# Down-projection end, softmax units and output projection reordered in a gated FFN plus two attention layers on one core

## The chip, the core and the metric

The kernel runs on one NeuronCore of a Trainium2 chip. The metric is the time of one execution on the device, in microseconds (us). Five engines work side by side and wait for each other through semaphores: TensorE (PE) does matmuls, VectorE (DVE) and ScalarE (ACT) elementwise work and reductions, GpSimd (POOL) a few set-ups, SyncE (SP) issues the loads. PE writes to PSUM (8 banks of 128 x 512 float32); DVE and ACT read it.

## What is computed

512 tokens of width 1024 go through a first block (a recurrent token mixer, then a gated FFN with a causal convolution) and then through two layers of three attention branches:

```python
# first block, FFN part
f = causal_dwconv(hn @ w_up) + b;  gate, up = split(f)
ffn = (gelu(gate) * up) @ w_down                  # 2816 -> 1024
h = h + rms_norm(ffn, post_ffn_g)
# each of two layers
h = rms(x, norm_g);  proj = h @ w_in
log_a = log_sigmoid(a_lr @ wa2 + ba) / 16         # 16 -> 256, decay of the linear attention
y_a = linear attention * silu(gz)
y_b = sparse attention (top keys by an indexer) * silu(bz)
y_c = (softmax(Q1 K1) - lambda softmax(Q2 K2)) V, normed, * silu(cz)
merged = sum of sigmoid(gate_b) * (y_b @ w_br[b]) over the three branches
x = x + merged @ w_out
```

## The kernel before

Every large matmul is done in float32r as three products: each operand is split into a high part and a low part (the rest), and high x high, low x high and high x low are summed in PSUM. So each weight panel (up to 128 x 2048 elements) goes through three steps: SP loads it to `w_raw`; ACT copies it to `w_hi` (`split_hi`, L347); DVE subtracts and writes `w_lo` (`split_lo`, L365). All three tiles have two slots, used in turn by the panel's number. `w_hi` of a panel can be written only after PE is done with the panel two before it, PE takes a panel only when its `w_lo` is there, and SP loads into a slot once the low part of its former panel is made.

The order of work on each engine is written out by hand, one function per engine and stage; an engine takes its list strictly in order. The helpers `high(p)` and `low(p)` put the two splits of panel p into ACT's and DVE's lists. The stages that matter here:

**FFN end** (`ffn`). The down projection has 11 panels. ACT, for each: `split_hi` of the panel, then the high part of the hidden values (`g hi`, L1776). DVE: `g lo` (L1820), then `split_lo`. The last two panels are worked by PE token tile by token tile (L1719), and a seam follows that norms the result and starts layer 0.

**Decay bias** (`layer`). The low-rank values stand in `lowrank_iw`, 24 rows: 16 of the decay, 8 index weights. For each of four token tiles PE multiplies the 16 rows by `gla_wa2` (L2236) and adds the bias by a matmul with one row of ones (L2237).

**Softmax loops** (`layer`). Two per layer, 16 units each (a head and a query tile of 128, with 4, 3, 2, 1 key tiles visible), first for the difference attention ("d"), then for the sparse one ("s"). PE, at unit u: transposes the probabilities of u, makes the logits of u + 2, computes one tile of a merge panel as filling, multiplies u's probabilities with the values. DVE: maximum of u + 1 (`softmax_max`), in the first loop one step of a top-k search, normalisation of u + 1 (`softmax_norm`), gating of a branch tile, and after odd units the low part of the panel two ahead. ACT: copy of the transposed probabilities (L2461), high parts at odd units, exponentials (L2447), head output (L2468). ACT keeps its functions in tables that have to be loaded on a change (ACT_TABLE_LOAD).

**Output projection** (`first_out`). `outs[0]` is the first of four panels of `w_out`; PE goes through it by rows of the merged values as their low parts (`merged lo`, L3021) come. ACT makes eight `merged hi` copies (L2659); the last two depend on the gating of the last merge panel by DVE (L2801, L2807).

```python
for i in range(2):
    gated(mergeB + 7, i)
    merged_lo(KT - 2 + i)
low(outs[1])
```

Of the kernel before, what the change touches and what calls it, by code (L numbers as in the profile page):

```python
# [72 lines left out]
SHARED = ("seam", "w raw", "w hi", "w lo", "w used")  # L73
# [267 lines left out]
def split_hi(act, m, g, n):  # L341

    act.wait_ge(*act.point(("w raw", g)))
    act.wait_ge(act.done, act.so_far())
    if g >= 2:
        act.wait_ge(act.sems["pe"], act.at(("w used", g - 2)))
    act.eng.activation(m.wh[:, g % 2, 0:n], m.raw[:, g % 2, 0:n], ACT.Copy).then_inc(act.done, 1)  # L347
    act.counted(("w hi", g))

# [1277 lines left out]
def ffn(m, A, done, sems, seam, after, base):  # L1627
# [120 lines left out]
    def scalar(E):  # L1748
        act = E.eng
        post_sum(E, m, seam, 0)  # L1750
        pre_sum(E, m, seam, 0)
        post_sum(E, m, seam, 1)
        split_hi(E, m, base, PANEL)
        pre_sum(E, m, seam, 1)
        seam_hi(E, m, seam, 0)
        post_sum(E, m, seam, 2)
        seam_hi(E, m, seam, 1)
        post_sum(E, m, seam, 3)
        split_hi(E, m, base + 1, PANEL)
        pre_sum(E, m, seam, 2)  # L1760
        pre_sum(E, m, seam, 3)
        seam_hi(E, m, seam, 2)
        seam_hi(E, m, seam, 3)
        for p in range(FT):
            E.wait_ge(act_done, E.so_far())
            if p >= 2:
                E.wait_ge(dve_done, E.at(("G", p - 2)))
            E.wait_ge(dve_done, E.at(("conv", p, 0)))
            act.activation(m.gel[:, p % 2, :], m.cgu[:, p % 2, 0, :], ACT.Gelu_apprx_tanh).then_inc(act_done, 1)
            E.counted(("gelu", p))  # L1770
            split_hi(E, m, base + p + 2, PANEL)
        for kk in range(2, DN):
            split_hi(E, m, down_base + kk, PANEL)
            E.wait_ge(act_done, E.so_far())
            E.wait_ge(dve_done, E.at(("G", 2 * kk + 1)))
            act.activation(m.gH[:, kk % 2, :, :], m.G[:, 2 * kk:2 * kk + 2, :], ACT.Copy).then_inc(act_done, 1)  # L1776
            E.counted(("g hi", kk))
        seam_table(E, m, after)

    def vector(E):  # L1780
# [36 lines left out]
        for kk in range(2, DN):  # L1817
            E.wait_ge(dve_done, E.so_far())
            E.wait_ge(act_done, E.at(("g hi", kk)))
            dve.tensor_tensor(m.gL[:, kk % 2, :, :], m.G[:, 2 * kk:2 * kk + 2, :], m.gH[:, kk % 2, :, :].bitcast(F32),  # L1820
                              ALU.subtract).then_inc(dve_done, 1)
            E.counted(("g lo", kk))
            split_lo(E, m, down_base + kk, PANEL)
# [12 lines left out]
RANK = 16  # L1836
TAU = 16.0
# [5 lines left out]
def lay_out_layers(nc, m):  # L1843
# [35 lines left out]
    m.lw = take("lowrank_iw", [RANK + IH, T], over=q + 24 * KB)  # L1879
# [10 lines left out]
    m.wa2 = take("gla_wa2", [RANK, 256], over=pt)  # L1890
    m.ba = take("gla_ba", [1, 256], over=pt + KB)
# [3 lines left out]
    m.sc = take("index_scores", [P, P * sum(range(2, TT + 1))])  # L1895
    m.later = m.bd
# [12 lines left out]
def layer(m, A, out, done, sems, l, base, seam, after):  # L1909
# [102 lines left out]
    def sync(E):  # L2012
        sp = E.eng

        def rows_in():
# [12 lines left out]
            sp.dma_start(m.wa2[:, :], A["gla_wa2_2"][l, :, :]).then_inc(small_loaded, 16)  # L2028
            sp.dma_start(m.ba[:, :], A["gla_ba_2"][l:l + 1, :]).then_inc(small_loaded, 16)
# [32 lines left out]
    def gpsimd(E):  # L2062
# [7 lines left out]
        if l == 0:  # L2070
            E.wait_ge(pe_done, E.before(None, ("y mean", JT - 1)))
            E.wait_ge(dve_done, E.before(None, ("conv", FT - 1, 1)))
            step(pool.affine_select(out=m.later[:, :], in_=m.later[:, :], compare_op=ALU.is_gt, fill=0.0, base=0,
                                    pattern=[[-1, P]], channel_multiplier=1), "later 3")
            for i in range(2):
                step(pool.memset(m.lamc[:, i, 0:1], LAMBDA[i]), ("lambda 0", i))
                step(pool.memset(m.lamc[:, i, 1:2], 1.0 - LAMBDA[i]), ("lambda 1", i))

    def tensor(E, banks):
# [148 lines left out]
        turn(E, m, banks, "turn iw", 6, "iw", [m.lw[:, P * t:P * t + P] for t in range(TT)],  # L2228
             rows=RANK + IH)
        E.wait_ge(*E.point("small"))  # L2230
        for g in range(2):
            o = start(("z", g), 4 + g, ("la", g))
            for q in range(2):
                t = 2 * g + q
                oo = o[:, 256 * q:256 * q + 256]
                pe.matmul(oo, m.lw[0:RANK, P * t:P * t + P], m.wa2[:, :], start=True, stop=False)  # L2236
                last = pe.matmul(oo, m.onesP[0:1, :], m.ba[:, :], start=False, stop=True)  # L2237
# [140 lines left out]
    def scalar(E):  # L2378
# [6 lines left out]
        def evac(p, i):  # L2385
# [5 lines left out]
            if p == lows:  # L2391
# [4 lines left out]
                ins = act.activation(m.lw[:, :], PS[64:64 + RANK + IH, b, :], ACT.Copy)  # L2396
# [202 lines left out]

        exps(0, "d", (0, 1), 64 ** -0.5)  # L2600
# [50 lines left out]
        for p in range(mergeB, mergeB + 7):  # L2651
# [4 lines left out]
        for j in range(KT):  # L2656
# [3 lines left out]
            E.counted(("merged hi", j))  # L2660
        high(outs[1])
        high(outs[2])
# [4 lines left out]
    def vector(E):  # L2667
# [280 lines left out]
        step(cz[1])  # L2948
        softmax_max(0, "d")
        softmax_norm(0, "d")  # L2950
        softmax_max(1, "d")
        softmax_norm(1, "d")
        for u in range(1, NU):
            p, i = mergeA + u // 2, u % 2
            if u + 1 < NU:
                softmax_max(u + 1, "d")
            top(18 + u, 19 + u)
# [4 lines left out]
            if i:  # L2962
                low(p + 2)
# [38 lines left out]
        for u in range(1, NU):  # L3002
            p, i = mergeC + u // 2, u % 2
            if u + 1 < NU:
                softmax_max(u + 1, "s")
                softmax_norm(u + 1, "s")
            if panels[p].name == "br":
                gated(p, i)
            if i:
                low(p + 2)  # L3010
# [19 lines left out]
        low(outs[0])  # L3030
        for j in range(KT - 2):
            merged_lo(j)
        for i in range(2):
            gated(mergeB + 7, i)
            merged_lo(KT - 2 + i)
# [103 lines left out]
```

## Time and profile before

| what | value |
|---|---|
| median of three timed runs | 2007.99 us (2002.96 to 2009.97) |
| profiled execution, its own time | 1997.83 us |
| its span | 1996.1 us |
| PE busy | 1918.2 us, 96% |
| weight loads on PE | 1543.2 us, 77% |
| DVE busy | 1144.9 us, 57% |
| ACT busy | 744.9 us, 37% |
| POOL busy | 54.2 us, 3% |
| 16 DMA engines, queue of the weights | 25.8% of their span, 159.00 MB |
| granted TensorE clock, mean | 0.989 of full |

The profile is one execution as the hardware recorded it; busy times are per engine and overlap. A line such as "745.72 0.47 PE L1719 ... [1.49 <-DVE w_lo L365]" gives the start, the length, the engine, the code line, the operation with what it writes and reads, and in brackets how long the engine was idle before it and which event ended that.

### The profile page before, as it was taken

What the parts mean: (1) busy time and instruction counts of PE and PEld (TensorE: products, weight loads), DVE (VectorE), ACT (ScalarE), POOL (GpSimd) and SP (SyncE); (2) the same over time, 40 slices, a digit from 0 to 9 for tenths busy, and PEclk for the clock granted to TensorE, in tenths of its full rate; (3) what the DMA queues carried; (4) which work ended last, traced back from release to release, by engine and by line L of the source; (5) the groups of instructions that cost most, each with busy time, mean ns of one, the idle gap of its engine ahead of it and who ended that gap; (6) DMA issues with size and microseconds to landing.
All of it is one profiled execution on the core that took longest, in us unless ns stands there. A gap on an engine that the chain in (4) does not pass through costs nothing.

```text
span 1996.1 us, 30217 instructions
## 1 busy us (share of the span) xinstructions
PE 1918.2 (96%) x12657; PEld 1543.2 (77%) x12657; DVE 1144.9 (57%) x1684; ACT 744.9 (37%) x1063; POOL 54.2 (3%) x75
## 2 busy tenths in 40 slices
PE   6989998899999999999999999999999999999998
PEld 4767775888888878787777778878778777778887
DVE  3674345476766236446687855454446678775533
ACT  5532422432222226433444334333543344334431
POOL 3000000310000000000000000000000000000000
PEclk9999998999999999999999999999999999999999
DMA  4221003233333232222222212233222312232232
GB/s 145 77 64 45 25 24 112 65 84 106 85 106 98 93 112 86 67 85 85 64 64 85 90 59 84 74 100 101 85 78 70 95 57 82 73 96 64 64 106 84
DMA packets 166034, 161.63 MB, mean 81 GB/s; under 512 B 13892, under 2 KB 150378, under 8 KB 165898
## 3 DMA queue, kind: packets, MB, share of 16 engines
q1 hardware_dynamic: 165200, 159.00, 25.8%
q8 instruction: 99, 1.62, 0.3%
q10 hardware_dynamic: 698, 0.71, 0.1%
q14 instruction: 37, 0.30, 0.0%
HBM read 157.59 MB, written 2.10 MB: 80 GB/s over the span
## 4 chain that ended last, share of the span: by engine, by line
PE 69%; DVE 6%; ACT 3%; issue 1%; ACTq 0%; DVEq 0%
PE psum L557 57%; PE psum L1719 5%; DVE w_lo L365 2%; PE psum L2203 1%; ACT w_hi L347 1%; PE psum L547 1%; PE psum L2160 1%; PE psum L2188 1%; DVE softmax_stats L2758 1%; ACT probs L2447 1%; PE psum L2180 1%; PE psum L495 1%; DVE h_lo L3021 0%; PE psum L504 0%; DVE probs L2789 0%
## 5 line engine op out<-in xcount | busy, mean ns | idle before, releaser
L557 PE MATMUL psum<-h_hi,w_hi 128*128 128x512 f32 (+2 forms) x1592 | 624.6, 392 | 15.9 <-DVE h_lo L429 7.4
L557 PE MATMUL psum<-h_lo,w_hi 128*128 128x512 f32 (+2 forms) x1592 | 607.8, 382 | 0.0
L557 PE MATMUL psum<-h_hi,w_lo 128*128 128x512 f32 (+2 forms) x1592 | 607.8, 382 | 0.0
L365 DVE TENSOR_TENSOR w_lo<-w_raw,w_hi 128x2048 fp32r<-128x2048 f32 (+2 forms) x147 | 306.7, 2086 | 367.4 <-ACT w_hi L347 365.0
L347 ACT ACTIVATE w_hi<-w_raw 128x2048 fp32r<-128x2048 f32 (+2 forms) x157 | 276.5, 1761 | 397.9 <-PE psum L557 318.9
L557 PEld LDWEIGHTS psum<-h_hi,w_hi 128*128 128x128 f32 (+1 forms) x1592 | 300.7, 189 | 96.0 <-issue 13.6
L557 PEld LDWEIGHTS psum<-h_hi,w_lo 128*128 128x128 f32 (+1 forms) x1592 | 300.7, 189 | 58.3
L557 PEld LDWEIGHTS psum<-h_lo,w_hi 128*128 128x128 f32 (+1 forms) x1592 | 301.3, 189 | 53.9
L557 PE MATMUL psum<-w_hi,h_hi 128*128 128x512 f32 (+1 forms) x512 | 183.3, 358 | 7.5 <-DVE w_lo L365 4.0
L557 PE MATMUL psum<-w_lo,h_hi 128*128 128x512 f32 (+1 forms) x512 | 179.9, 351 | 0.0
L557 PE MATMUL psum<-w_hi,h_lo 128*128 128x512 f32 (+1 forms) x512 | 179.8, 351 | 0.0
L557 PEld LDWEIGHTS psum<-w_hi,h_hi 128*128 128x128 f32 x512 | 97.8, 191 | 36.0 <-issue 11.4
L557 PEld LDWEIGHTS psum<-w_hi,h_lo 128*128 128x128 f32 x512 | 97.8, 191 | 12.8
L557 PEld LDWEIGHTS psum<-w_lo,h_hi 128*128 128x128 f32 x512 | 97.9, 191 | 11.7
L557 PE MATMUL psum<-y_hi,w_hi 128*128 128x512 f32 x192 | 80.2, 418 | 0.0
L2447 ACT ACTIVATE probs<-psum,softmax_stats 128x128 f32<-128x128 f32 (+3 forms) x72 | 36.1, 506 | 113.8 <-DVE softmax_stats L2773 113.8
L557 PE MATMUL psum<-y_hi,w_lo 128*128 128x512 f32 x192 | 75.2, 392 | 0.0
L557 PE MATMUL psum<-y_lo,w_hi 128*128 128x512 f32 x192 | 75.2, 391 | 0.0
L1804 DVE TENSOR_SCALAR ffn_conv<-psum,ffn_cols 128x512 f32<-128x512 f32 x44 | 35.6, 810 | 63.3 <-PE psum L557 62.2
L1719 PE MATMUL psum<-w_hi,ffn_hi 128*128 128x512 f32 x176 | 68.8, 391 | 2.0 <-DVE w_lo L365 1.5
L1719 PE MATMUL psum<-w_lo,ffn_hi 128*128 128x512 f32 x176 | 68.5, 389 | 0.0
L1719 PE MATMUL psum<-w_hi,ffn_lo 128*128 128x512 f32 x176 | 68.5, 389 | 0.0
(339 smaller groups left out, 2128.5 us busy)
## 6 DMA issues: line engine op xcount, KB each, us to landing
w_raw<-in_w_in_dram SPq DMA_DIRECT2D x170, 512.0 KB, 4.5
w_raw<-in_w_up_dram SPq DMA_DIRECT2D x44, 512.0 KB, 4.7
w_raw<-in_w_out_dram SPq DMA_DIRECT2D x24, 512.0 KB, 4.5
w_raw<-in_w_br_dram SPq DMA_DIRECT2D x48, 256.0 KB, 2.9
w_raw<-in_w_down_dram SPq DMA_DIRECT2D x22, 512.0 KB, 4.3
x_first<-in_x_dram SPq DMA_DIRECT2D x4, 512.0 KB, 5.2
x_tokens<-in_x_dram SPq DMA_DIRECT2D x4, 512.0 KB, 6.6
out_dram<-x_tokens SPq DMA_DIRECT2D x4, 512.0 KB, 2.6
```

Of the source, the lines that this page charges most:

```text
L347: act.eng.activation(m.wh[:, g % 2, 0:n], m.raw[:, g % 2, 0:n], ACT.Copy).then_inc(act.done, 1)
L365: eng.eng.tensor_tensor(m.wl[:, g % 2, 0:n], m.raw[:, g % 2, 0:n], m.wh[:, g % 2, 0:n].bitcast(F32), ALU.subtract).then_inc(eng.done, 1)
L495: last = pe.eng.matmul(out[q, :], m.ind[:, kind, q], x[:, j, :], start=begin, stop=end, skip_group_check=True)
L547: last = pe.eng.transpose(m.PS[0:n, bank, rows * i:rows * i + rows], b, m.ident[at:at + rows, at:at + rows])
L557: last = pe.eng.matmul(out, a(k), b(k), start=(opens and k == 0 and i == 0), stop=(k == kt - 1 and i == 2), skip_group_check=ks is not None)
L1719: last = pe.matmul(PS[:, 2 * t + n, :], g[:, kk % 2, k, tt], w[:, k, cc], start=(kk == 0 and k == 0 and i == 0), stop=(kk == DN - 1 and k ...
L1804: dve.tensor_scalar(c, z, tap[2], bias, ALU.mult, ALU.add).then_inc(dve_done, 1)
L2160: pe.matmul(o[:, 0:vis], m.Q[r, h // 2, P * i:P * i + P], m.ikf[r, 0:vis], start=True, stop=True).then_inc(pe_done, 1)
L2180: last = pe.matmul(o[:, 0:vis], m.Q[r, h, P * i:P * i + P], m.K[r, h, 0:vis], start=True, stop=True)
L2188: pe.matmul(o[:, 0:vis], m.Q[:, h, P * i:P * i + P], m.K[:, h, 0:vis], start=True, stop=True).then_inc(pe_done, 1)
L2203: last = pe.matmul(o[:, 0:P], m.V[:, k, P * h:P * h + P], m.PT[:, u % 2, P * k:P * k + P], start=(k == 0), stop=(k == i))
L2447: ins = act.activation(dst, src, ACT.Exp, bias=m.st[:, u % 2, 2 + c:3 + c], scale=scale, accum_out=m.st[:, u % 2, 4 + c:5 + c])
```

## The change

- FFN: the weights of the last down panel are split in two halves on ACT and on DVE (`split_hi_halves`, `split_lo_halves`), and on ACT the high part of the hidden values goes ahead of them; it gets a wait of its own for the down panel two before it.
- Layers, decay bias: `lowrank_iw` and `gla_wa2` get 32 rows and places of their own. Rows 24 to 31 of the first are ones; of the second, row 24 is the bias and the others beyond 16 are zero. One matmul in place of two. POOL clears both once, in layer 0, and SP waits for that.
- First softmax loop: an exponential of two columns is put right behind the last evacuation, so that the table is loaded there; DVE waits for it. The low part of panel `mergeA + 1` moves behind the first maximum.
- Both loops: low parts move from after odd units into the following even unit, between maximum and normalisation.
- Output projection: first panel in halves; the high part of the second panel moves ahead of the last two merged copies, and DVE makes both last gatings before the last two low parts.

```diff
+def split_hi_halves(act, m, g, n):
+    act.wait_ge(*act.point(("w raw", g)))
+    if g >= 2:
+        act.wait_ge(act.sems["pe"], act.at(("w used", g - 2)))
+    for half in range(2):
+        c = slice(n // 2 * half, n // 2 * (half + 1))
+        act.wait_ge(act.done, act.so_far())
+        act.eng.activation(m.wh[:, g % 2, c], m.raw[:, g % 2, c], ACT.Copy).then_inc(act.done, 1)
+        act.counted(("w hi", g) if half else ("w hi half", g))
+def split_lo_halves(dve, m, g, n):
+    for half in range(2):
+        c = slice(n // 2 * half, n // 2 * (half + 1))
+        dve.wait_ge(dve.done, dve.so_far())
+        dve.wait_ge(dve.sems["act"], dve.at(("w hi", g) if half else ("w hi half", g)))
+        dve.eng.tensor_tensor(m.wl[:, g % 2, c], m.raw[:, g % 2, c], m.wh[:, g % 2, c].bitcast(F32),
+                              ALU.subtract).then_inc(dve.done, 1)
+        dve.counted(("w lo", g) if half else ("w lo half", g))
...
         for kk in range(2, DN):
-            split_hi(E, m, down_base + kk, PANEL)
+            if kk < DN - 1:
+                split_hi(E, m, down_base + kk, PANEL)
             E.wait_ge(act_done, E.so_far())
             E.wait_ge(dve_done, E.at(("G", 2 * kk + 1)))
+            E.wait_ge(pe_done, E.at(("dn mm", kk - 2)))
             act.activation(m.gH[:, kk % 2, :, :], m.G[:, 2 * kk:2 * kk + 2, :], ACT.Copy).then_inc(act_done, 1)
             E.counted(("g hi", kk))
+        split_hi_halves(E, m, down_base + DN - 1, PANEL)
...
-            split_lo(E, m, down_base + kk, PANEL)
+            if kk < DN - 1:
+                split_lo(E, m, down_base + kk, PANEL)
+        split_lo_halves(E, m, down_base + DN - 1, PANEL)
...
-            sp.dma_start(m.wa2[:, :], A["gla_wa2_2"][l, :, :]).then_inc(small_loaded, 16)
-            sp.dma_start(m.ba[:, :], A["gla_ba_2"][l:l + 1, :]).then_inc(small_loaded, 16)
+            if l == 0:
+                E.wait_ge(pool_done, E.at("low ones"))
+            sp.dma_start(m.wa2[0:RANK, :], A["gla_wa2_2"][l, :, :]).then_inc(small_loaded, 16)
+            sp.dma_start(m.wa2[LOWS:LOWS + 1, :], A["gla_ba_2"][l:l + 1, :]).then_inc(small_loaded, 16)
...
+            step(pool.memset(m.wa2[:, :], 0.0), "low zeros")
+            step(pool.memset(m.lw[:, :], 1.0), "low ones")
...
-                pe.matmul(oo, m.lw[0:RANK, P * t:P * t + P], m.wa2[:, :], start=True, stop=False)
-                last = pe.matmul(oo, m.onesP[0:1, :], m.ba[:, :], start=False, stop=True)
+                last = pe.matmul(oo, m.lw[:, P * t:P * t + P], m.wa2[:, :], start=True, stop=True)
...
+        E.wait_ge(act_done, E.so_far())
+        act.activation(m.st[:, 0, 2:4], m.eps[:, :], ACT.Exp).then_inc(act_done, 1)
+        E.counted("exp table")
         exps(0, "d", (0, 1), 64 ** -0.5)
...
-        for p in range(mergeB, mergeB + 7):
+        for p in range(mergeB, mergeB + 6):
...
-        for j in range(KT):
+        gate(mergeB + 6, 0)
+        gate(mergeB + 6, 1)
+        split_hi_halves(E, m, base + outs[0], size(outs[0]))
+        for j in range(KT - 2):
+            merged_hi(j)
         high(outs[1])
+        merged_hi(KT - 2)
+        merged_hi(KT - 1)
...
-        step(cz[1])
+        E.wait_ge(act_done, E.at("exp table"))
         softmax_max(0, "d")
+        low(mergeA + 1)
         softmax_norm(0, "d")
...
             if u + 1 < NU:
                 softmax_max(u + 1, "d")
+            if i == 0:
+                low(p + 1)
             top(18 + u, 19 + u)
             if u + 1 < NU:
                 softmax_norm(u + 1, "d")
             if panels[p].name == "br":
                 gated(p, i)
-            if i:
-                low(p + 2)
+        low(bq[1])
...
-        low(outs[0])
+        split_lo_halves(E, m, base + outs[0], size(outs[0]))
         for j in range(KT - 2):
             merged_lo(j)
         for i in range(2):
             gated(mergeB + 7, i)
-            merged_lo(KT - 2 + i)
+        merged_lo(KT - 2)
+        merged_lo(KT - 1)
```

## Rows read from the trace of the kernel before

**Rows 1.** The page, busy us of each engine with its share of the span.
```profile
PE 1918.2 (96%) x12657; PEld 1543.2 (77%) x12657; DVE 1144.9 (57%) x1684; ACT 744.9 (37%) x1063; POOL 54.2 (3%) x75
```
**Rows 2.** Timeline of PE, FFN end: start, length, what, idle before.
```profile
743.84 0.39 PE L1719 MATMUL psum<-w_lo,ffn_hi 128*128 128x512 f32 x1
745.72 0.47 PE L1719 MATMUL psum<-w_hi,ffn_hi 128*128 128x512 f32 x1 [1.49 <-DVE w_lo L365]
```
**Rows 3.** Timeline of ACT, FFN end.
```profile
738.91 1.92 ACT L347 ACTIVATE w_hi<-w_raw 128x2048 fp32r<-128x2048 f32 x1 [7.87 <-PE psum L1719]
740.86 1.06 ACT L1776 ACTIVATE ffn_hi<-ffn_hidden 128x1024 fp32r<-128x1024 f32 x1
...
743.23 0.20 ACT L400 ACTIVATE row_stats<-eps 128x1 f32<-128x1 f32 x1
```
**Rows 4.** Groups by shape, 984:1084, DVE low part of 128x1024: busy, mean ns.
```profile
L365 DVE TENSOR_TENSOR w_lo<-w_raw,w_hi 128x1024 fp32r<-128x1024 f32 x4 | 4.9, 1226 | 7.0 <-ACT w_hi L347 6.9
```
**Rows 5.** Timeline of PE, decay matmuls of layer 0 and the panel behind.
```profile
790.16 0.59 PE L2236 MATMUL psum<-gla_wa,lowrank_iw 16*128 16x256 f32 x2
790.59 0.59 PE L2237 MATMUL psum<-gla_ba,ones 1*128 1x256 f32 x2
791.69 0.79 PE L557 MATMUL psum<-h_hi,w_hi 128*128 128x512 f32 x1 [0.51 <-DVE w_lo L365]
```
**Rows 6.** Timelines of DVE, ACT and PE, start of the first softmax loop.
```profile
986.81 0.17 DVE L2750 MEMSET psum<- 64x128 f32 x1
...
988.51 1.28 ACT L2447 ACT_TABLE_LOAD   x1 [2.50 <-DVE softmax_stats L2773]
...
992.95 0.66 PE L547 MATMUL psum<-ident,probs 128*128 128x128 f32 x4 [1.37 <-DVE probs L2789]
```
**Rows 7.** Timelines of DVE and PE, unit 2 of that loop.
```profile
1003.83 2.29 DVE L365 TENSOR_TENSOR w_lo<-w_raw,w_hi 128x2048 fp32r<-128x2048 f32 x1 [3.12 <-ACT w_hi L347]
...
1008.92 0.35 DVE L2789 SCALAR_TENSOR_TENSOR probs<-probs,softmax_stats 128x128 f32<-128x128 f32 x1
...
1009.77 0.27 PE L547 MATMUL psum<-ident,probs 128*128 128x128 f32 x1
```
**Rows 8.** Timelines of DVE and PE, end of that loop.
```profile
1076.15 2.29 DVE L365 TENSOR_TENSOR w_lo<-w_raw,w_hi 128x2048 fp32r<-128x2048 f32 x1 [2.27 <-ACT w_hi L347]
...
1079.40 0.69 DVE L2712 MAX8 top<-index_scores 128x8 f32<-128x512 f32 x1
...
1081.04 0.71 PE L2203 MATMUL psum<-probs_t,v_toks 128*128 128x128 f32 x4 [1.56 <-ACT probs_t L2461]
1081.90 0.33 PE L547 MATMUL psum<-ident,probs 128*128 128x128 f32 x1
```
**Rows 9.** Timeline of PE, end of the second loop.
```profile
1263.91 0.71 PE L2203 MATMUL psum<-probs_t,v_toks 128*128 128x128 f32 x4 [0.43 <-ACT probs_t L2461]
```
**Rows 10.** Timelines of ACT, DVE and PE, output projection of layer 0.
```profile
1326.51 1.92 ACT L347 ACTIVATE w_hi<-w_raw 128x2048 fp32r<-128x2048 f32 x1
...
1330.86 4.32 DVE L3021 TENSOR_TENSOR h_lo<-merged,h_hi 128x512 fp32r<-128x512 f32 x6
...
1331.69 0.47 PE L557 MATMUL psum<-w_hi,h_hi 128*128 128x512 f32 x1 [0.52 <-DVE h_lo L3021]
...
1336.72 0.63 ACT L2659 ACTIVATE h_hi<-merged 128x512 fp32r<-128x512 f32 x1 [4.31 <-DVE merged L2807]
...
1344.86 0.47 PE L557 MATMUL psum<-w_hi,h_hi 128*128 128x512 f32 x1 [2.00 <-DVE w_lo L365]
```
**Rows 11.** Windows of PE: stretch, its us, PE busy, granted clock, DMA share, GB/s.
```profile
788.00:791.40 3.40, 3.18 (x15) 1.00 0.00 0
791.40:794.80 3.40, 3.11 (x7) 0.50 0.59 175
...
1402.40:1409.20 6.80, 6.80 (x17) 0.50 0.68 229
...
1695.90:1699.30 3.40, 3.40 (x11) 0.50 0.00 1
```

More of the change, by code:

```diff
@@ L70, in __init__ @@
         self.w = sum(c[2] for c in pieces)
-SHARED = ("seam", "w raw", "w hi", "w lo", "w used")
+SHARED = ("seam", "w raw", "w hi half", "w hi", "w lo half", "w lo", "w used")
 class Steps:
@@ L1836 @@
 RANK = 16
+LOWS = RANK + IH
 TAU = 16.0
@@ L1878, in lay_out_layers @@
     m.ikf = take("ik_feats", [P, T], over=q + 8 * KB)
-    m.lw = take("lowrank_iw", [RANK + IH, T], over=q + 24 * KB)
     o = at[0]
@@ L1889, in lay_out_layers @@
     m.rn3 = take("norm_rows3", [P, T], over=pt)
-    m.wa2 = take("gla_wa2", [RANK, 256], over=pt)
-    m.ba = take("gla_ba", [1, 256], over=pt + KB)
     m.lam_in = take("lambda_in", [P, 4, 64], over=pt + 2 * KB)
@@ L1895, in lay_out_layers @@
     m.sc = take("index_scores", [P, P * sum(range(2, TT + 1))])
+    m.lw = take("lowrank_iw", [LOWS + LOWS // 3, T])
+    m.wa2 = take("gla_wa2", [LOWS + LOWS // 3, 256])
     m.later = m.bd
@@ L2227, in tensor @@
         E.wait_ge(act_done, E.at(("Levac", lows, 0)))
-        turn(E, m, banks, "turn iw", 6, "iw", [m.lw[:, P * t:P * t + P] for t in range(TT)],
+        turn(E, m, banks, "turn iw", 6, "iw", [m.lw[0:LOWS, P * t:P * t + P] for t in range(TT)],
              rows=RANK + IH)
@@ L2395, in evac @@
                 E.counted("ik high")
-                ins = act.activation(m.lw[:, :], PS[64:64 + RANK + IH, b, :], ACT.Copy)
+                if l == 0:
+                    E.wait_ge(pool_done, E.at("low ones"))
+                ins = act.activation(m.lw[0:LOWS, :], PS[64:64 + LOWS, b, :], ACT.Copy)
             elif panels[p].tokens:
@@ L2655, in scalar, with merged_hi @@
             high(p + 2)
-        for j in range(KT):
+        def merged_hi(j):
             E.wait_ge(act_done, E.so_far())
@@ L3005, in vector @@
                 softmax_max(u + 1, "s")
+            if i == 0:
+                low(p + 1)
+            if u + 1 < NU:
                 softmax_norm(u + 1, "s")
@@ L3008, in vector @@
                 gated(p, i)
-            if i:
-                low(p + 2)
+        low(mergeB + 1)
         for h in range(NH):
```

## The prediction

> **What bounds the kernel now.** I read the page's busy times first: TensorE (PE) is busy for 1918.2 of a 1996.1 us span [rows 1]. So only two things can shorten the run: fewer PE instructions on its path, or shorter pauses between them. I then went through PE's timeline for pauses in the three stages that the change touches, and at each one looked at ACT and DVE in the same microseconds for the step that ended it. The pauses sit at handovers: end of the down projection, start and end of each softmax loop, and the output projection. Each gap, as shown, is 0.16 us short of what it costs: a matmul is drawn 0.39 us long, but in the steady stream the next one starts after 0.23 us [rows 2]. I count gap + 0.16.
>
> **End of the FFN.** The last down panel (10) needs two things from ACT: the high part of its weights (1.92 us), then that of the hidden values (1.06). DVE follows with two low parts, the second a 128x2048 of 2.29 us (as in [rows 7]). PE starts at 745.72 after 1.49 idle, so 1.65 lost [rows 2, 3]. After the change ACT starts at the same 738.91 (the new wait, on down panel 8, is the event that released ACT before): hidden high part to 739.97, weight halves to 741.06 and 742.14, each costed as the 128x1024 copy of 1.06 [rows 3]. DVE: hidden low part 740.07 to 741.30, first half 741.33 to 742.56, second half, which must wait for ACT's second half, 742.60 to 743.83, at 1.23 us each [rows 4]. PE could start at 743.97. Its stream before ends with a start at 743.84, so the natural next start is 744.07 [rows 2]: the pause goes, with 0.1 us to spare. Gain 1.65 (bounds 0 and 1.65; I take all of it, since every duration has a row of its own shape). Halving costs 0.20 us on ACT and 0.17 on DVE, already in these times. The seam behind it hangs on this panel's result, so it moves along. ACT's root table load is next and has over 3 us until its first use.
>
> **Decay bias as a row.** Per layer, four matmuls with K=1 go; each of the eight took 0.43 us from start to start, so 1.7 us of PE work per layer. But PE then waits 0.51 us anyway for the low part of the next panel, whose high part could only begin when the panel before was used [rows 5]. PE would merely arrive 1.7 us earlier and wait 2.2. In layer 1 the last of the eight ends just as that low part is ready, so again nothing is freed. Value 0; bounds 0 and 3.5 us for both layers, and nearer 0 because the waiting step has no link to the bias. The two memsets on POOL, and SP's wait for them in layer 0, lie behind the up panels and ahead of the seam, in time when POOL has nothing else; the rows and weights queued behind SP's wait are asked for later. The zero rows cost nothing in streaming: PE's time here is by columns. I have no row for K=32; bounds are the K=1 and K=16 times, both 0.43.
>
> **Exponential table early (start of the first softmax loop, in both layers).** Now: ACT evacuates until 986.01, idles 2.50, loads the table only after DVE's maximum (1.28), then exponentials; PE waits 1.37 [rows 6]. After: load 986.03 to 987.31, dummy exponential 0.20 (as the one-column operation of [rows 3]), 987.53. DVE's maximum writes the same statistics tile and so now waits for this: it starts at about 987.60 instead of 986.81 [rows 6], 0.79 later, and the 1.30 behind it goes. Net 0.51, twice 1.0. Queued behind DVE's new wait: maximum, a weight low part (1.23), the normalisation. That low part moves between maximum and normalisation and runs 989.25 to 990.47, while ACT's exponentials run to about 990.7, so it is covered; were it not, it would cost its 1.23. Bounds -1.2 and 1.53 per layer.
>
> **Low parts inside a unit (both softmax loops).** Order on DVE was low part, next maximum, normalisation; it becomes maximum, low part, normalisation. The low part waits for ACT anyway (3.12 us idle before it [rows 7]), and the maximum, 0.8 us, fits in that idle. Inside the loop PE has no pause to win. At the end of the first loop it has: DVE does the low part (begun at 1076.15, right behind ACT's high part) until 1078.44, then the maximum and its small steps until 1079.40; ACT's exponentials wait for that, the transposed probabilities come late, and PE pauses 1.56 before the values of unit 14; unit 15's transpose at 1081.90 then follows DVE's normalisation [rows 8]. After: the maximum is done before the low part, ACT is free from 1076.05, unit 14's values start without pause, and unit 15's normalisation ends 0.96 earlier, which is what remains as PE's limit. Unit 15's own path behind it is unchanged. I take 0.92 per layer, 1.8 in all (bounds 0 and 1.72 per layer). In the second loop the same pause is 0.43, cost 0.59 [rows 9], and goes whole: there the normalisation is ready when the values end. 1.2 for both layers.
>
> **Output projection.** PE pauses 0.52 before its first panel and 2.00 before its second [rows 10], that is 0.68 and 2.16. First: ACT's high part in halves from 1326.51 ends at 1328.66 instead of 1328.43, but DVE starts on the first half at 1327.67, ends both at 1330.14 and the first merged low part (0.72) at 1330.86; PE can go at 1331.0, its natural start being 1331.03. Gain 0.66. Second: the panel's high part stood behind all eight merged copies on ACT, though ACT idled 4.31 us before the seventh [rows 10]. Now it goes into this idle, 1332.65 to 1334.57 (its buffer is free when panel 7 of the merge ends at about 1331.2). DVE: five more merged low parts to 1334.5, four gating steps of 0.72 to 1337.4, low parts 7 and 8 to 1338.9, weight low part to 1341.3. PE ends the first panel at 1342.1. Gain 2.16, with 0.8 us to spare (bounds 0 and 2.16). Both layers: 5.6.
>
> **Sum.** 1.65 + 2 x (0 + 0.51 + 0.92 + 0.59 + 0.66 + 2.16) = 11.3 us. The profiled execution took 1997.83 (span 1996.1 and 1.7 around it), so 1986.5 in its terms. The three timed runs lie higher, 2002.96 to 2009.97 with median 2007.99, 10.2 above it; I carry the difference over: 1996.7.
>
> **The clock.** TensorE's granted clock was 1.00 in 788.0:791.4 and 0.50 in the 3.4 us behind it [rows 11]: the lower of its two levels, 1.2 for 2.4 GHz, and 1.7 us lost. Before this fall PE ran small matmuls almost without a gap (3.18 of 3.40 us busy).
> The Trainium skill (TensorE: Matmul & The Clock Gate, "What's actually happening") says that the engine is throttled by default and only activity lifts this, with idleness bringing it back. By that, the 2.2 us idle that the bias edit leaves speaks against the change; the trace agrees only in part, since the engine here was busy, if with few rows.
>
> **Rivals.**
> A. The falls get fewer, since pauses at loop ends shrink. The clock stood at the lower level after the decay matmuls of both layers (3.4 and 6.8 us) and after the first softmax loop of layer 1 (3.4) [rows 11]: half of 13.6 is 6.8. Then -18.1, 1990. For it: one of the three follows exactly a pause that shrinks. Against: two follow the decay matmuls, whose stretch keeps its length.
> B. The falls get more or longer: PE idle instead of working ahead of the panel, in both layers, for one or two such stretches each, 1.7 us a time: 3.4 to 6.8 back, so -4.5 to -7.9, 2000 to 2003.5. For it: idle comes in. Against: the low-activity stretch (787.1 to 791.7) is as long as before.
> C. The handovers without margin don't pay (FFN end, table, first output panel: 0.1, 0.5 and 0.03 us are small against a late semaphore): then only 2 x (0.92 + 0.59 + 2.16) = 7.3 stays, 2000.7. For it: two margins of 0.1 or less. Against: a missed margin costs only what it misses.
> D. Slower: the low part now stands in front of the normalisation, and PE's transpose waits for that. In unit 2, normalisation ended at 1009.27 and the transpose came at 1009.77: 0.5 us slack [rows 7]. If the 2.29 us low part began that much later than now, four such panels a loop and four loops would cost 16 x 1.8 = 29 us, net +17, 2025. It decides from 1.2 us of delay per unit (0.5 slack + 11.3/16). Against: the low part begins when ACT's high part is ready, in both orders; only if the maximum's logits were late would it be delayed, and they are issued two units ahead.
>
> **Numbers.** Forecast 0.60 (its own range 1992 to 2001), A 0.12, B 0.12, C 0.11, D 0.05. What a measurement of this kernel can tell from no change is about 0.3%, 6 us. Faster by more: forecast, A, most of C and half of B, less a little for the 7 us between equal runs: 0.81. Within: 0.14. Slower: 0.05. Range 1989 to 2003.5: A below, B and C above, D left out.
>
> **What would show it.** PE's gap of 1.49 before the last down panel and those of 0.52 and 2.00 before the output panels gone; 1.37 down to about 0.85 at the first loop's start; 1.56 at its end replaced by about 1.0 before unit 15's transpose; the gap behind the decay matmuls up from 0.51 to 2.2 with the next panel no earlier. Wrong, if DVE's normalisations end later inside the loops, or if the first output panel starts on time and the second still waits, or if the granted clock falls in more places than three behind the FFN.

## The result and the profile after

| | before | this change |
|---|---|---|
| median of 4 runs, us | 2006.88 (2002.96 to 2009.97) | 1984.8 (1983.99 to 1985.71) |
| profiled execution: time, span | 1997.83, 1996.1 | 1984.06, 1982.0 |
| mean granted clock, profiled | 0.989 | 0.989 |

The ratio is 0.99, interval 0.9879 to 0.992. The forecast of 1996.7 us was 11.9 too high, and the time lies below its range (1989). The two profiled executions differ by 14.1 us of span where the sum said 11.3.

The page after, for [rows 1]: busy us of each engine, and the chain that ended last by engine.

```profile
PE 1911.6 (96%) x12641; PEld 1540.9 (78%) x12641; DVE 1145.3 (58%) x1687; ACT 746.2 (38%) x1068; POOL 56.5 (3%) x77
...
PE 75%; DVE 2%; ACT 1%; issue 0%; ACTq 0%; DVEq 0%
```

On the page of before that last line reads PE 69%, DVE 6%, ACT 3%. So DVE and ACT held 9 per cent of the chain, and 3 are left. That is where the chain runs, not what was gained: 6 per cent of the span would be 120 us.

PE's timeline after (start, length, what, idle before), in the order of [rows 2, 5, 6, 8, 9, 10]:

```profile
743.89 0.39 PE L1742 MATMUL psum<-w_lo,ffn_hi 128*128 128x512 f32 x1
744.12 0.39 PE L1742 MATMUL psum<-w_hi,ffn_hi 128*128 128x512 f32 x1
...
787.99 1.97 PE L2268 MATMUL psum<-gla_wa,lowrank_iw 32*128 32x256 f32 x8
...
792.20 0.80 PE L580 MATMUL psum<-h_hi,w_hi 128*128 128x512 f32 x1 [2.25 <-DVE w_lo L388]
...
993.11 0.33 PE L570 MATMUL psum<-ident,probs 128*128 128x128 f32 x1 [0.90 <-DVE probs L2834]
...
1078.91 0.61 PE L2235 MATMUL psum<-probs_t,v_toks 128*128 128x128 f32 x4
1079.54 0.33 PE L570 MATMUL psum<-ident,probs 128*128 128x128 f32 x1
1080.29 0.49 PE L2235 MATMUL psum<-probs_t,v_toks 128*128 128x128 f32 x2 [0.43 <-ACT probs_t L2494]
...
1260.95 0.61 PE L2235 MATMUL psum<-probs_t,v_toks 128*128 128x128 f32 x4
...
1327.99 0.47 PE L580 MATMUL psum<-w_hi,h_hi 128*128 128x512 f32 x1
...
1338.96 0.39 PE L580 MATMUL psum<-w_hi,h_hi 128*128 128x512 f32 x1
```

This view leaves out the brackets where the idle time is under 0.15 us. The pauses of 1.49, 1.56, 0.43, 0.52 and 2.00 us are gone (the 0.43 shown at 1080.29, before the values of unit 15, is another one, and before has it too), 1.37 is 0.90, and 0.51 behind the decay matmuls is 2.25. Unit 15's transpose (1079.54) follows unit 14's values at once: the rest of 1.0 us that the prediction left there isn't there. The end of the FFN and the output projection, from ACT's side and then from DVE's, for [rows 3, 10]:

```profile
739.64 1.06 ACT L1801 ACTIVATE ffn_hi<-ffn_hidden 128x1024 fp32r<-128x1024 f32 x1 [7.87 <-PE psum L1742]
740.79 2.16 ACT L359 ACTIVATE w_hi<-w_raw 128x1024 fp32r<-128x1024 f32 x2
...
1323.47 2.16 ACT L359 ACTIVATE w_hi<-w_raw 128x1024 fp32r<-128x1024 f32 x2
1325.66 3.96 ACT L2696 ACTIVATE h_hi<-merged 128x512 fp32r<-128x512 f32 x6
1329.70 1.92 ACT L347 ACTIVATE w_hi<-w_raw 128x2048 fp32r<-128x2048 f32 x1
1333.02 0.63 ACT L2696 ACTIVATE h_hi<-merged 128x512 fp32r<-128x512 f32 x1 [1.40 <-DVE merged L2852]
```

```profile
740.80 1.23 DVE L1846 TENSOR_TENSOR ffn_lo<-ffn_hidden,ffn_hi 128x1024 fp32r<-128x1024 f32 x1 [5.38 <-ACT ffn_hi L1801]
742.06 2.48 DVE L369 TENSOR_TENSOR w_lo<-w_raw,w_hi 128x1024 fp32r<-128x1024 f32 x2
...
1324.63 2.48 DVE L369 TENSOR_TENSOR w_lo<-w_raw,w_hi 128x1024 fp32r<-128x1024 f32 x2 [9.04 <-ACT w_hi L359]
1327.15 4.33 DVE L3070 TENSOR_TENSOR h_lo<-merged,h_hi 128x512 fp32r<-128x512 f32 x6
```

The hidden values come first, the weights in two copies behind them, and DVE starts on the first half while ACT makes the second. The second output panel's high part now fills ACT's idle time.

**Where the 14.1 us are.** I cut PE's timeline at the same named instructions in every profiled execution. In brackets: us of the stretch at the lower granted clock, where there are any.

| stretch, us | before | after | gain |
|---|---|---|---|
| start to first down matmul | 639.9 (30.7) | 640.6 (30.7) | -0.7 |
| down projection | 123.31 | 121.60 | 1.71 |
| seam, to decay of layer 0 | 24.26 | 25.76 (3.4) | -1.50 |
| decay to first softmax loop, both layers | 394.52 (10.2) | 394.59 (10.2) | -0.07 |
| first softmax loop, both layers | 197.26 | 191.48 | 5.78 |
| first to second loop, both layers | 188.70 (3.4) | 187.08 | 1.62 |
| second softmax loop, both layers | 178.28 | 176.90 | 1.38 |
| second loop to next layer or end | 249.86 | 243.95 | 5.91 |

What is left of the difference of the spans, once the clock's falls (-1.50, +1.62), the untouched first stretch and the 0.07 of the fourth are set aside, is 15.0: 1.71 + 2 x 2.99 + 1.38 + 5.91, with the first loop of layer 1 counted as that of layer 0.

### The profile page after: what moved, and what is told of

Read it like the earlier page. It is cut to its first block, busy times and chain, and to the rows that moved or that the text cites. A ratio compares the mean times of both kernels' runs of the same rounds, so it can differ in the third digit from the quotient of the medians.

```text
span 1982.0 us, 30195 instructions
## 1 busy us (share of the span) xinstructions
PE 1911.6 (96%) x12641; PEld 1540.9 (78%) x12641; DVE 1145.3 (58%) x1687; ACT 746.2 (38%) x1068; POOL 56.5 (3%) x77
## 3 DMA queue, kind: packets, MB, share of 16 engines
q8 instruction: 99, 1.62, 0.3%
## 4 chain that ended last, share of the span: by engine, by line
PE 75%; DVE 2%; ACT 1%; issue 0%; ACTq 0%; DVEq 0%
PE psum L580 62%; PE psum L1742 5%; PE psum L2235 2%; PE psum L570 1%; PE psum L2212 1%; PE psum L2192 1%; PE psum L2220 1%; DVE w_lo L388 1%; PE psum L518 1%; ACT w_hi L347 1%; PE psum L527 0%; PE psum L2316 0%; DVE h_lo L452 0%; DVE ffn_normed L465 0%; PE psum L2301 0%; DVE x_tokens L469 0%
## 5 line engine op out<-in xcount | busy, mean ns | idle before, releaser
L388 DVE TENSOR_TENSOR w_lo<-w_raw,w_hi 128x2048 fp32r<-128x2048 f32 (+2 forms) x144 | 299.8, 2082 | 285.6 <-ACT w_hi L347 282.9
L347 ACT ACTIVATE w_hi<-w_raw 128x2048 fp32r<-128x2048 f32 (+2 forms) x154 | 270.7, 1758 | 390.9 <-PE psum L580 320.0
L2512 ACT ACTIVATE squares<-psum 128x512 f32<-128x512 f32 x48 | 28.7, 598 | 109.2 <-PE psum L580 108.8
```

The lines of the kernel that those rows point to most:

```text
L388: eng.eng.tensor_tensor(m.wl[:, g % 2, 0:n], m.raw[:, g % 2, 0:n], m.wh[:, g % 2, 0:n].bitcast(F32), ALU.subtract).then_inc(eng.done, 1)
L2512: act.activation(m.sq3[:, 2 * (r % 2) + i, :], PS[:, bank(p, i), :], ACT.Tanh, scale=0.5).then_inc(act_done, 1)
```

## The experiments

Every kernel below was timed against the kernel before on the same chip. Since the run time follows the mean granted clock of its run, I also give each kernel's distance to before at equal clock: one straight line of time against mean clock through all timed runs, with a level of its own for each kernel (slope 17.8 us per 0.01 of clock, residual 1.57 us). There were 73 runs of before beside these kernels and 12 of its repetition, 1998.0 to 2014.9 us; all 85 count as one kernel. Two limits of this measure: before's own level differs by up to 0.9 us between the three series (lowest in the one with the table, the FFN end, the third run of the change and the change without the bias row), and a fall of the clock that a kernel itself avoids is taken out with the rest.

**Before and after once more.** No edit; the change as it stands in the second and, on another occasion, a third series.

> The kernel before, unchanged, timed and profiled again. Open is why its timed runs lay 5 to 12 us above its profiled execution, while those of the changed kernel lie within 2 us of theirs. Theory 1 (the excess is a state of those runs or of that chip, not of the program): here its times come out near 1998, equal to its profile within 2 us, and the changed kernel is 12 to 15 us below it. Theory 2 (the program itself loses more clock in most executions than in the one profiled): timed runs at 2003 to 2010 again, and in single runs more time at the lower of the two clock levels.

> The whole change, timed beside the kernel before on one chip. Theory 1: 12 to 15 us faster (the spans of the two traces differ by 14.1). Theory 2: about 20 to 22 us faster, 1984 to 1986 in all runs.

> The whole change a third time, to see what a handful of runs can be worth. Theory 1 (the program gains 15.0 us at an equal granted clock, and the rest of the first result, 7 us, was the draw of the clock in four runs against four): the runs spread over 1984 to 1998 with their mean clock between 0.982 and 0.989, and fitted against the clock they lie 15 us below the kernel before. Theory 2 (the change itself makes falls of the clock rarer, and so gains 20 or more on the whole): all runs at 1984 to 1987, mean clock 0.988, while the kernel before keeps its 0.985.

Before against itself: ratio 1.0006 (0.9987 to 1.0025), its median 2006.77 (1999.0 to 2014.7), which speaks for theory 2; for the change theory 1 held both times. The change: 1990.1 us (1983.8 to 1997.3) against 2003.59, ratio 0.9927 (0.9902 to 0.9952); the third time 1988.74 against 2003.03, ratio 0.9918 (0.99 to 0.9937). At equal clock it is 14.6 and 14.9 us faster (±1.3 each), and 14.9 in the four runs of the result. So the change is worth 15 us, 0.75%. By this line the rest of the 22 us between the medians of the result is which executions were caught. This windows view shows PE busy, matmul count, granted clock, DMA share and GB/s over the first 640 us, which the change doesn't touch: before, after, then these two kernels.

```profile
0.00:640.00 640.00, 586.64 (x6064) 0.98 0.27 80
```

```profile
0.00:640.00 640.00, 586.41 (x6061) 0.98 0.27 80
```

```profile
0.00:640.00 640.00, 585.17 (x6024) 0.96 0.26 78
```

```profile
0.00:640.00 640.00, 583.74 (x6002) 0.95 0.26 77
```

The first of the two kernels here is before again, its span 2008.2 us at a mean clock of 0.983; 12 us of it lie above the 1996.1 of the same program in the other execution, 9.1 of them in these 640 us. The second is the change, 1995.0 us at 0.982. With the same edits in both pairs, the lower clock took 30.7 us of this stretch in the first pair and 47.8 and 58.0 in the second.

**Only the output projection.** The two functions for halves, and:

```diff
+        gate(mergeB + 6, 0)
+        gate(mergeB + 6, 1)
+        split_hi_halves(E, m, base + outs[0], size(outs[0]))
+        for j in range(KT - 2):
+            merged_hi(j)
...
-        low(outs[0])
+        split_lo_halves(E, m, base + outs[0], size(outs[0]))
```

> Only the edits of the output projection in both layers (first panel in halves, second panel's high part ahead of the last two merged copies, gatings ahead of the low parts). By the sum of the prediction 2 x 2.82 = 5.6 us less than before; the gaps of 0.52 and 2.00 gone. Rival (gain of the whole lies in fewer falls of the clock): 5.6 us in the trace, but more in the timed runs.

1998.9 us, ratio 0.9965 (0.9951 to 0.9979), 7.4 faster at equal clock (±1.0). In the trace the stage is 2.95 us shorter in layer 0 and 2.86 in layer 1 (130.87 and 113.18 for 133.82 and 116.04): 5.8, the predicted 5.6 and a little. The time at equal clock reads 1.6 more than the trace, outside its error; I follow the trace, and the cause of the difference is open. (The four parts alone add up to 16.3 at equal clock, ±2.3, beside 15.0 in the traces.)

**Only the order inside the units.** Both loops as in the change from their second unit on, nothing else (the low part behind the first maximum belongs to the kernel with the table, below):

```diff
                 softmax_max(u + 1, "d")
+            if i == 0:
+                low(p + 1)
             top(18 + u, 19 + u)
...
-            if i:
-                low(p + 2)
+        low(bq[1])
```

> Only the low parts moved inside a unit, in both softmax loops of both layers. The prediction had 2 x (0.92 + 0.59) = 3.0 us. The traces before and after differ by 2.5 and 0.6 us per layer in these stretches, so 6.2 us if the excess belongs to this edit (DVE's whole list in the loop runs ahead, ACT's high part of the panel behind the loop with it); 3.0 if the excess comes from the earlier table load.

2001.82 us, ratio 0.9979 (0.9961 to 0.9996), 6.1 faster at equal clock (±1.0). The first loop takes 96.19 us in place of 98.73, the second 88.45 in place of 89.14: 2.5 where 0.92 was predicted, and 0.69 for 0.59. With layer 1, whose first loop gained 2.35, these are 6.3. The stretch behind the first loop of layer 1 has no fall of the clock.

**Only the last low part of each loop.** The prediction's mechanism for the end of the loop names one low part, the last. On before, that one alone is put behind the maximum, in both loops:

```diff
                 softmax_max(u + 1, "d")
+            if u == NU - 2:
+                low(p + 1)
...
-            if i:
+            if i and u != NU - 3:
                 low(p + 2)
```

> Of the unit order only one low part per loop is moved: that of the panel behind the loop, from after unit 13 to behind the maximum of unit 15. Theory 1 (the prediction's: only that maximum leaves the path): the first loop 0.92 us shorter than before, 98.73 to 97.8, the second 0.59 to 0.69. Theory 2 (the six earlier moves let ACT's exponentials run beside DVE's low parts all through the loop, and DVE's whole list comes 1.4 us early at its end): this edit alone gives 0.9 in the first loop and the other 1.6 of the 2.54 belong to the earlier moves. Rival: already this edit gives 2 us or more, and the earlier moves nothing.

The loop takes 97.80 us in place of 98.73: 0.93, the 0.92 of the prediction to the hundredth. The second loop takes 88.45, its whole gain. So the other 1.6 us of the first loop come from the six low parts before it. PE's row at the end has the pause of about 1.0 before unit 15's transpose that the prediction expected of the whole change:

```profile
1081.49 0.33 PE L547 MATMUL psum<-ident,probs 128*128 128x128 f32 x1 [1.06 <-DVE probs L2789]
```

2000.59 us, ratio 0.9972 (0.9954 to 0.999), 3.9 faster at equal clock (±1.1), of which the trace shows 2 x (0.93 + 0.69) = 3.2.

**Only the exponential table.** The dummy exponential, DVE's wait for it ahead of the first maximum, and the low part of `mergeA + 1` moved behind that maximum. The two edits were not tried apart.

```diff
+        E.wait_ge(act_done, E.so_far())
+        act.activation(m.st[:, 0, 2:4], m.eps[:, :], ACT.Exp).then_inc(act_done, 1)
+        E.counted("exp table")
...
-        step(cz[1])
+        E.wait_ge(act_done, E.at("exp table"))
         softmax_max(0, "d")
+        low(mergeA + 1)
```

> Only the early exponential table and the low part behind the first maximum. By the prediction 0.51 us per layer, 1.0 in all: the first softmax loop 98.7 to 98.2 us long. Rival: the remainder of what that loop gained (3.0 us, of which the unit order alone gave 2.5) is 0.5 and the two simply add; if instead this edit alone gives 1 us or more per layer, they share a gain.

2004.27 us, ratio 1.0008 (0.9995 to 1.0022), at equal clock 1.7 faster (±1.0), and 0.9 against the runs of before in its own series alone. The first loop takes 98.11 us in place of 98.73, and 98.10 for 98.53 in layer 1: 0.6 and 0.4, the 0.51 of the prediction. PE's pause is 0.90 us:

```profile
997.49 0.66 PE L547 MATMUL psum<-ident,probs 128*128 128x128 f32 x4 [0.90 <-DVE probs L2792]
```

**Only the end of the FFN.** The hunks of the down projection.

```diff
+            E.wait_ge(pe_done, E.at(("dn mm", kk - 2)))
...
+        split_hi_halves(E, m, down_base + DN - 1, PANEL)
```

> Only the last down panel in halves. Prediction 1.65 us: the gap of 1.49 before it gone and the stretch from the first down matmul to the seam's first transposes 123.3 to 121.6. Rival: the margin of 0.1 us is not met and 0.1 to 0.3 of it stay.

2001.71 us, ratio 0.9988 (0.9971 to 1.0005), at equal clock 1.1 faster (±1.0), and 0.4 against its own series. By their ratios neither this kernel nor the one with the table can be told from before; what each is worth is read from the traces. The down projection takes 121.60 in place of 123.31. The seam has the change's fall of the clock, 1.5 us, so this execution gave nearly all of it back.

**The change without the bias row.** Two matmuls, K=16 and K=1, as before; all else as in the change.

```diff
-                last = pe.matmul(oo, m.lw[:, P * t:P * t + P], m.wa2[:, :], start=True, stop=True)
+                pe.matmul(oo, m.lw[0:RANK, P * t:P * t + P], m.wa2[:, :], start=True, stop=False)
+                last = pe.matmul(oo, m.onesP[0:1, :], m.ba[:, :], start=False, stop=True)
```

> The change without the decay bias as a row. Theory 1 (worth nothing, the next panel starts when its low part is there): the same time as the whole change at an equal clock, within 1 us, and the stretch from the decay matmuls to the first softmax loop as long. Theory 2 (the 2.2 us that PE idles there cost a fall of the clock that would not come otherwise): 1.7 to 6.8 us less time than the whole change and fewer us at the lower clock level behind the decay matmuls.

1988.85 us, ratio 0.9926 (0.9904 to 0.9949); at equal clock 15.4 faster than before, the change in the same series 14.9 (±1.3 each). The bias row is worth nothing that these runs can tell, as predicted. The clock fell behind the decay matmuls here too, with PE at work all through; the windows view, 2 stretches:

```profile
795.00:798.40 3.40, 3.40 (x15) 2.84 (x14) 2.30 (x3) 3.28 (x3) 0.00 (x0) 0.84 0.00 0
798.40:805.20 6.80, 6.80 (x19) 4.90 (x18) 3.14 (x5) 6.64 (x8) 0.00 (x0) 0.58 0.80 277
```

Behind the stretch's length the columns are PE, PEld, DVE, ACT and POOL busy with their counts, then the granted clock, the DMA share and GB/s.

**The output projection without halves.** On "only the output projection": the second panel's high part stays early, the first is again one copy.

```diff
-        split_hi_halves(E, m, base + outs[0], size(outs[0]))
+        high(outs[0])
...
-        split_lo_halves(E, m, base + outs[0], size(outs[0]))
+        low(outs[0])
```

> The output projection as changed, but its first panel split whole. By the prediction the halves are worth 0.66 us per layer and the second panel 2.16, so the gap of 0.52 is back and the stretch from the end of the sparse loop to the decay matmuls is 131.5 us instead of 130.85 (133.8 before). Rival: whole splitting pushes DVE's later steps back too, and a gap before the second panel appears.

The stage takes 131.55 us in place of 130.87, and the pause of before is back:

```profile
1335.57 0.47 PE L580 MATMUL psum<-w_hi,h_hi 128*128 128x512 f32 x1 [0.52 <-DVE h_lo L3053]
```

The halves are worth 0.68 a layer and the early high part 2.3, the predicted 0.66 and 2.16. 1997.57 us, ratio 0.9973 (0.9952 to 0.9994).

**One step further.** On the change: the table load ahead of the weight copy that it stood behind, and halves for the panel behind the decay matmuls.

```diff
-        step(cz[1])
-
+        evac(cz[1], 0)
+        evac(cz[1], 1)
         E.wait_ge(act_done, E.so_far())
         act.activation(m.st[:, 0, 2:4], m.eps[:, :], ACT.Exp).then_inc(act_done, 1)
         E.counted("exp table")
+        high(cz[1] + 2)
...
-        high(2)
+        split_hi_halves(E, m, base + 2, size(2))
...
-        low(2)
+        split_lo_halves(E, m, base + 2, size(2))
```

> The whole change and two more edits that its trace points to. (a) On ACT the last evacuation and the exponential table go ahead of the high part of the next panel: 1.06 us less on the chain that ends PE's pause at the loop's start; the pause of 0.90 there goes, the first loop 95.74 to 94.7. (b) The panel behind the decay matmuls is split in halves on ACT and DVE: 1.92 + 2.29 on the chain become 1.06 + 2 x 1.23, so PE's pause of 2.25 falls to about 1.6. Together 2 x (0.65 + 1.0) = 3.3 us less than the whole change at an equal clock. Rivals: for (a) the low part of that panel now ends later and delays the normalisation; for (b) the pause is followed by as long a time at the lower clock, and nothing is left.

1983.7 us, ratio 0.9884 (0.9862 to 0.9907): the best of all, 18.2 us faster than before at equal clock (±1.3) and 3.4 faster than the change (±1.5). The first loop takes 94.63 us for 95.74, with no pause at its start, and PE waits 1.55 us behind the decay matmuls instead of 2.25. The two rivals did not come: the loop is shorter by what was expected, and the time at the lower clock behind the decay matmuls is 6.8 us over both layers. ACT's timeline at the loop's start, then PE's behind the decay matmuls:

```profile
994.40 0.60 ACT L2435 ACTIVATE z_feats<-psum 128x512 f32<-128x512 f32 x1 [4.84 <-PE psum L580]
995.01 1.28 ACT L2634 ACT_TABLE_LOAD   x1
...
996.61 1.06 ACT L347 ACTIVATE w_hi<-w_raw 128x1024 fp32r<-128x1024 f32 x1
...
998.33 0.69 ACT L2480 ACTIVATE probs<-psum,softmax_stats 128x512 f32<-128x512 f32 x1 [0.66 <-DVE softmax_stats L2819]
```

```profile
801.66 0.58 PE L580 MATMUL psum<-h_hi,w_hi 128*128 128x512 f32 x1 [1.55 <-DVE w_lo L369]
```

## Why the prediction was wrong in size

**Right, by its own numbers.** The end of the FFN: 1.65 predicted, 1.71 measured. PE's start at 744.12 is its natural one, 0.23 us behind the start before it. Second softmax loop: 0.59 and 0.69. First output panel: 0.66 and 0.68. Second: 2.16 and about 2.3. Table: 0.51 and 0.4 to 0.6. Bias row: 0 and nothing measurable; the pause of 0.51 became 2.25 (2.2 predicted), and the next panel starts no earlier. Rival C falls, since in the traces every handover with a small margin paid. Rival D falls: DVE's low part in unit 2 still starts when ACT's high part is there, and the normalisation ends before PE wants it. DVE's timeline after, for [rows 7] (the loop's step u = 2, which normalises unit 3):

```profile
1004.00 2.29 DVE L388 TENSOR_TENSOR w_lo<-w_raw,w_hi 128x2048 fp32r<-128x2048 f32 x1 [1.27 <-ACT w_hi L347]
...
1008.16 0.35 DVE L2834 SCALAR_TENSOR_TENSOR probs<-probs,softmax_stats 128x128 f32<-128x128 f32 x1
```

It ends at 1008.51 and PE's transpose comes at 1009.94, 1.4 us of slack where before had 0.5. The wait for ACT fell from 3.12 to 1.27, because the maximum fills it.

**The step that failed in the sum** is "Inside the loop PE has no pause to win", and with it "unit 15's normalisation ends 0.96 earlier, which is what remains as PE's limit". In the first loop 0.92 was mis-sized: it is 2.5 a layer, 3.2 us in all. The rest of the 3.7 us that the sum lacked is small excesses of the other terms. The chain of waits of before shows why. Its pieces, in order of time (start, length, what):

```profile
1064.84 1.24 DVE w_lo L365
...
1066.16 0.18 DVE psum L2750
1066.36 0.97 DVE softmax_stats L2758
...
1068.09 0.76 ACT probs L2447 x3
...
1070.38 0.18 DVE psum L2750
1070.58 0.70 DVE softmax_stats L2758
...
1073.55 0.50 ACT probs_t L2461
...
1074.13 1.93 ACT w_hi L347
...
1076.15 2.30 DVE w_lo L365
```

From 1058.6 to 1081.9 no piece of it is PE's, and back to 1034.6, about the middle of the loop, only 1.8 us are (1056.81 to 1058.61). DVE and ACT take turns, each idle for much of the other's work: low part, maximum, exponentials, normalisation, next maximum. The same chain of the change is PE's all through this stretch, until 1079.5:

```profile
1065.13 5.65 PE psum L580 x24
1070.79 0.89 PE psum L2235 x8
...
1072.43 3.01 PE psum L580 x12
...
1076.33 2.74 PE psum L580 x12
1079.07 0.46 PE psum L2235 x4
```

In the timelines, unit 13's maximum began at 1066.16 and begins at 1063.00, its exponentials had waited 4.04 us and wait 2.60, and the high part behind the loop began at 1074.13 and begins at 1072.69, though the loop itself starts 0.6 us later in this trace. That the earlier moves carry this is shown by the kernel with the last low part alone (0.93) against the one with all of them (2.5). What they change on DVE is its wait ahead of the 128x2048 low parts, 2.3 us in before and 1.3 in the kernel with the unit order alone; first before, then that kernel:

```profile
1027.88 2.29 DVE L365 TENSOR_TENSOR w_lo<-w_raw,w_hi 128x2048 fp32r<-128x2048 f32 x1 [2.27 <-ACT w_hi L347]
```

```profile
1037.82 2.29 DVE L365 TENSOR_TENSOR w_lo<-w_raw,w_hi 128x2048 fp32r<-128x2048 f32 x1 [1.28 <-ACT w_hi L347]
```

The maximum, which used to follow, now lies in that wait. So the normalisations of units 3, 7, 11 and 15 end 0.56, 1.41, 1.88 and 2.53 us earlier than in before, counted from the loop's first matmul. PE feels little of this at first. The starts of its transposes, in us from that matmul:

| unit | 6 | 7 | 8 | 11 | 12 | 14 | 15 |
|---|---|---|---|---|---|---|---|
| before | 44.50 | 49.23 | 56.13 | 73.26 | 80.17 | 92.22 | 97.76 |
| last low part alone | 44.50 | 49.22 | 56.12 | 73.25 | 80.16 | 92.20 | 96.83 |
| all low parts | 44.50 | 49.19 | 56.02 | 72.75 | 79.58 | 91.63 | 95.22 |

Up to unit 6 the moves are worth nothing to PE. From unit 7 to unit 14 they save 0.6 us in pauses too short for the timeline's brackets. The largest is this one of before, where the values start 0.48 us behind the matmul ahead of them and the steady stream has 0.23:

```profile
1056.33 0.39 PE L557 MATMUL psum<-y_hi,w_lo 128*128 128x512 f32 x1
1056.81 0.71 PE L2203 MATMUL psum<-probs_t,v_toks 128*128 128x128 f32 x4
```

The other 1.95 us lie behind unit 14: the 0.9 that was predicted, and 1.0 more because DVE comes early enough that the pause before unit 15's transpose goes too. I had read PE's pauses and the operation that ended each, and for the middle of the loop only that PE had none.

**The step that failed in the forecast** is "I carry the difference over". The 10.2 us between three runs and the profiled execution are no property of the kernel. Over 73 runs before lies anywhere from 1998.0 to 2014.9, and the profiled 1997.83 is below them all. The 11.9 us by which the forecast was too high are: 3.7 that the sum lacked (15.0 for 11.3), 1.1 from before's median (2006.88 with its fourth run, not 2007.99), and 7.1, the rest. I put this rest down to the clock: the four runs of the change had a mean clock of 0.9885, and the line puts 2006.88 us of before at 0.9845. The clocks of those four runs of before aren't recorded, so this last part is worked out and not measured. Against the medians of later series (1990.1 and 1988.7) the forecast was 6.6 and 8.0 too high; the first lies inside the range, the second 0.3 below it.

**Rivals A and B.** One of the falls that A names went, and a fall that neither rival names came in, in the seam; that the two nearly cancel in the two profiled executions (1.62 and 1.50 us) is chance. The falls behind the first loop (1.6 us each) appear in one or both layers of before, of its repetition and of the four kernels that keep the low part ahead of the maximum (only output projection, only table, only FFN, output without halves), 9 times behind 12 such loops, and never behind the 14 loops of the seven executions that move it, the last one or all. So this fall goes with the end of the loop; that is a count of executions, and no run isolated what in it decides. The fall in the seam (1.5 us) appears in the change and its repetitions and not in before, but also with the table or the output projection changed alone, which touch nothing before it, and it is missing in the change without the bias row; it isn't the change's doing. B did not come: behind the decay matmuls the time at the lower clock was 10.2 us over both layers in before and after alike, and in the thirteen profiled executions it was 6.8 to 13.6, with 13.6 only in three that keep the decay bias as before. The pause of 2.25 us did not make it longer, nor was it needed for it: the kernel without the bias row had no pause in layer 0 and 10.2 us too. The windows after, for [rows 11]:

```profile
788.10:791.50 3.40, 1.86 (x9) 1.00 0.00 0
791.50:794.90 3.40, 2.70 (x6) 0.60 0.48 140
```

The Trainium skill (TensorE: Matmul & The Clock Gate, "What's actually happening") says that idleness brings the throttled state back. This trace agrees for the change, where the fall follows a pause; the kernel without the bias row differs, since there PE was busy for 3.40 of 3.40 us up to its fall and into it, with small matmuls.

## What to carry to other kernels

Where two engines prepare operands in turn, look at the chain of waits through the middle of a loop, even if the matrix engine shows no pause there: a chain made only of the other two is a debt that comes due at the loop's end, and moving an operation that one of them does into its wait for the other pays there. Here it paid PE nothing up to unit 6, and most of its worth came at the end. A pause shorter than the difference between a matmul's drawn length and the distance of two starts (0.39 and 0.23 us here) isn't to be seen as idle time at all; compare the starts of the same matmul in two traces. Work that nothing waits for soon belongs behind the step that starts the other engine's turn, not ahead of it. To forecast a time, compare executions at equal granted clock; three or four runs of a kernel of 2 ms say less of a change of 0.7% than the sum over its timeline does.

## What the hardware showed that I had not expected

- Runs of one kernel on one core of one chip spread by 17 us (1998.0 to 2014.9) and follow the clock that they were granted. Most of this can be in one stage: 30.7 to 58.0 us of the first 640 at the lower level in the traces, in executions whose program is the same up to there.
- A decay matmul with 32 rows costs what one with 1 or 16 rows did. Four of them (two records each) lie in 1.97 us; with 0.59 for the length of the last from [rows 5] that is (1.97 - 0.59) / 3 = 0.46 from start to start. Before's first four start at 787.48, 787.99, 788.43 and 788.86, 0.46 apart in the mean as well: the first takes 0.51, the others 0.43.
